# Row gathers over 128 partitions instead of 96 in a two-layer encoder with a product-key expert stage

## What is computed

```python
u = jnp.take(u_tab, idx, axis=0)
act = jax.nn.gelu(jnp.einsum('td,thkd->thk', hb, u))
v = jnp.take(v_tab, idx, axis=0)
return jnp.einsum('thk,thkd->td', gate * act, v)
```

## Time and profile before

| what | value |
|---|---|
| median of 3 runs | 2128.72 us (2105.6, 2128.72, 2135.84) |
| profiled execution, its own time | 2104.95 us |
| its span in the profile | 2103.2 us |
| granted TensorE clock, mean | 0.965 |
| DMA moved | 525.69 MB, mean 250 GB/s |

### The profile page before, as it was taken

How to read it: one execution, slowest core, us unless ns; L and a number is a source line. 1 busy time by engine, 2 the same in 40 slices (tenths; PEclk the granted TensorE clock), 3 DMA queues, 4 the chain that set the end, 5 groups by cost and what they waited for, 6 DMA issues and landing times.

```text
span 2103.2 us, 32369 instructions
## 1 busy us (share of the span) xinstructions
PE 1719.7 (82%) x11548; PEld 1612.4 (77%) x11548; DVE 1224.8 (58%) x2667; ACT 526.5 (25%) x1404; POOL 776.2 (37%) x704
## 2 busy tenths in 40 slices
PE   8999998889966666658999999978799766666667
PEld 6889997779865655657988899978788766666567
DVE  5857986757755444443037668958667644444442
ACT  6854123434400000000047652134444100000000
POOL 6446243334443333331045453333344433333330
PEclk9999999999987988788999999999999999999999
DMA  7250899999999999999831325999999999999996
GB/s 278 81 201 2 269 306 291 292 289 312 309 277 271 281 272 268 274 275 292 279 137 70 132 81 190 287 296 289 289 311 309 294 286 288 289 289 286 279 281 198
DMA packets 143986, 525.69 MB, mean 250 GB/s; under 512 B 18208, under 2 KB 21792, under 8 KB 141472
## 3 DMA queue, kind: packets, MB, share of 16 engines
q1 hardware_dynamic: 86336, 322.57, 50.3%
q0 software_dynamic: 57568, 202.15, 34.9%
HBM read 523.60 MB, written 1.05 MB: 249 GB/s over the span
## 4 chain that ended last, share of the span: by engine, by line
DMA 57%; PE 28%; DVE 10%; ACT 2%; issue 2%; POOL 1%; SPq 0%; DVEq 0%; ACTq 0%; POOLq 0%
PE ps L590 27%; DMA ring<-in_peer_v 25%; DMA nat<-in_peer_v 11%; DMA nat<-in_peer_u 9%; DMA ring<-in_peer_u 8%; DMA grid<-in_u_rows,lists 4%; PE ps L587 1%; DVE grid L1556 1%; DMA grid<-in_w_in 1%; POOL gath_a L574 1%; DVE ab L1528 0%; DVE grid L1516 0%; DVE lists L1525 0%; DVE lists L1520 0%; DVE lists L1532 0%
## 5 line engine op out<-in xcount | busy, mean ns | idle before, releaser
L590 PE MATMUL ps<-grid,ring 128*128 128x160 f32 (+1 forms) x4096 | 632.7, 312 | 175.3 <-DMA ring<-in_peer_v 140.4
L590 PE MATMUL ps<-grid,nat 128*128 128x160 f32 (+1 forms) x4096 | 631.1, 312 | 171.7 <-DMA nat<-in_peer_v 141.2
L590 PEld LDWEIGHTS ps<-grid,ring 128*128 128x128 f32 x4096 | 589.9, 197 | 211.0 <-issue 161.3
L590 PEld LDWEIGHTS ps<-grid,nat 128*128 128x128 f32 x4096 | 588.9, 197 | 207.6 <-issue 172.0
L1612 DVE SCALAR_TENSOR_TENSOR grid<-grid,amount 96x1024 f32<-96x1024 f32 x128 | 163.9, 1281 | 188.5 <-DMA grid<-in_peer_v,lists 188.5
L1612 DVE SCALAR_TENSOR_TENSOR grid<-gath_a,amount,grid 96x1024 f32<-96x1024 f32 x126 | 161.4, 1281 | 188.1 <-DMA gath_a<-in_peer_v,lists 188.1
L574 POOL DMA_INDIRECT gath_a<-in_u_rows,lists x128 | 146.9, 1148 | 280.6 <-DVE dots L1600 207.6
L553 POOL TENSOR_TENSOR wl<-grid,wh 128x512 fp32r<-128x512 f32 (+2 forms) x128 | 142.6, 1140 | 210.4 <-PE ps L590 112.7
L574 POOL DMA_INDIRECT grid<-in_u_rows,lists x128 | 144.7, 1130 | 200.9 <-DVE dots L1600 186.3
L574 POOL DMA_INDIRECT gath_a<-in_peer_v,lists x128 | 119.7, 935 | 232.8 <-DVE grid L1612 209.3
L574 POOL DMA_INDIRECT grid<-in_peer_v,lists x128 | 115.7, 904 | 235.0 <-DVE grid L1612 221.9
(11 more groups left out here) (190 smaller groups left out, 1778.3 us busy)
## 6 DMA issues: line engine op xcount, KB each, us to landing
nat<-in_peer_u SPq DMA_DIRECT2D x128, 512.0 KB, 20.6
ring<-in_peer_u SPq DMA_DIRECT2D x128, 512.0 KB, 20.2
nat<-in_peer_v SPq DMA_DIRECT2D x128, 512.0 KB, 26.4
ring<-in_peer_v SPq DMA_DIRECT2D x128, 512.0 KB, 26.3
grid<-in_peer_wq SPq DMA_DIRECT2D x8, 2048.0 KB, 10.7
grid<-in_w_out SPq DMA_DIRECT2D x2, 4096.0 KB, 13.1
grid<-in_w_in SPq DMA_DIRECT2D x3, 2048.0 KB, 16.5
grid<-in_w_in SPq DMA_DIRECT2D x24, 256.0 KB, 14.4
```

The source lines that it names most:

```text
L590: return nc.tensor.matmul(dst, a, b, start=first, stop=last)
```

## The change

Each gather now fills all 128 partitions. Of the 128 picks of each of the 96 tokens, the first `NR` = 96 are gathered on the token's own partition as before. The last 32 are handed to partitions 96 to 127 (`helpers`): helper partition 96 + i takes the 32 last picks of token i in gathers 0 to 31, of token 32 + i in gathers 32 to 63, of token 64 + i in gathers 64 to 95. So there are 96 gathers of 128 rows for u and 96 for v in a layer, in place of 128 and 128 of 96 rows.

For this the row numbers of the last 32 picks are copied to the helpers (three copies at the end of the picks), the tokens' `xs` rows are copied to the helpers before dots 0, 32 and 64, the gate values likewise in `weigh`, and after additions 31, 63 and 95 the helpers' sums are copied back and added to `x` (`give_back`), the helpers' `acc` being cleared in between. `EARLY_DOTS` stays 24; two dots a round follow in the first 36 rounds of the gate loop and none in the last four.

```diff
+NR = NPK * NS // P
+NH = P - NS
 # gathers (POOL)
-  nc.gpsimd.indirect_dma_start(gath[m % OCT][own, :], None, u_rows if m < NPK else v_rows, bass.IndirectOffsetOnAxis(
-      ap=lists[own, 3, m % NPK:m % NPK + 1].bitcast(U32), axis=0)).then_inc(gath_in[m % OCT], 16)
+  nc.gpsimd.indirect_dma_start(gath[m % OCT], None, u_rows if m < NR else v_rows, bass.IndirectOffsetOnAxis(
+      ap=lists[:, 3, m % NR:m % NR + 1].bitcast(U32), axis=0)).then_inc(gath_in[m % OCT], 16)
-for m in range(2 * NPK):
+for m in range(2 * NR):
 # routing(64) (DVE)
-  v.tensor_copy(lists[own, 3, mine].bitcast(U32), lists[own, 3, mine]).then_inc(picked, 1)
+  ch.step(v.tensor_copy(lists[own, 3, mine].bitcast(U32), lists[own, 3, mine]))
+  for j in range(NS // NH):
+      ins = v.tensor_copy(lists[helpers, 3, j * NH:j * NH + NH].bitcast(U32), lists[j * NH:j * NH + NH, 3, NR:NPK].bitcast(U32))
+  ins.then_inc(picked, 1)
 # dots and additions (DVE)
+def helped(j):
+    if j:
+        dve.wait_ge(gath_used, past[gath_used] + j * NH)
+    ch.step(v.tensor_copy(xs[helpers, :], xs[j * NH:j * NH + NH, :]))
 def dot(n):
+    if n % NH == 0:
+        helped(n // NH)
+def weigh():
+    ch.before()
+    for j in range(NS // NH):
+        ch.did(v.tensor_copy(amount[helpers, j * NH:j * NH + NH], lists[j * NH:j * NH + NH, 0, NR:NPK]))
+    ch.did(v.tensor_copy(amount[own, :], lists[own, 0, 0:NR]))
+    dve.wait_ge(acts_ready, past[acts_ready] + 1)
+    ch.before()
+    ch.step(v.tensor_tensor(amount[:, :], amount[:, :], acts[:, :], ALU.mult))
+def give_back(j):
+    of = slice(j * NH, j * NH + NH)
+    dve.wait_ge(gath_used, past[gath_used] + NR + (j + 1) * NH)
+    ch.step(v.tensor_copy(xs[of, :], acc[helpers, :]))
+    if j < NS // NH - 1:
+        ch.did(v.memset(acc[helpers, :], 0.0))
+    ch.step(v.tensor_tensor(x[of, 0, :], x[of, 0, :], xs[of, :], ALU.add))
 def add_row(n):
+    if n % NH == NH - 1:
+        give_back(n // NH)
 # the gate loop and after it
   for i in range(2):
-      dot(EARLY_DOTS + 2 * m + i)
+      if EARLY_DOTS + 2 * m < NR:
+          dot(EARLY_DOTS + 2 * m + i)
       times_gelu(NA + 2 * m + i, m + 1)
-for n in range(EARLY_DOTS + 2 * NG4, NPK):
-    dot(n)
-dve.wait_ge(acts_ready, past[acts_ready] + 1)
-ch.step(v.tensor_tensor(amount[own, :], acts[own, :], lists[own, 0, 0:NPK], ALU.mult))
-for n in range(NPK):
+weigh()
+for n in range(NR):
     add_row(n)
```

More of the change, by code:

```diff
@@ L204, in build @@
         ikt, jkt, nwkt = (sb(name, [P, SEQ]) for name in ("ikt", "jkt", "nwkt"))
-        dots, acts, amount = (sb(name, [P, NPK]) for name in ("dots", "acts", "amount"))
+        dots, acts, amount = (sb(name, [P, NR]) for name in ("dots", "acts", "amount"))
         ps = ctx.enter_context(nc.psum_tensor("ps", [P, 8, 512], F32))
@@ L256, in build @@
         stat = [ps[:, 3, 384 + 32 * i:416 + 32 * i].rearrange("p (t n) -> p t n", t=NT) for i in range(3)]
-        own = slice(0, NS)
+        own, helpers = slice(0, NS), slice(NS, P)
         xf = part(NK * DT, KD * DT).rearrange("p (k t) -> p k t", k=KD)
@@ L343, in build @@
                 (NK, "prod_done act_stored y_done"),
-                (2 * NPK, "gath_used"),
-                (32 * NPK // OCT, " ".join(f"gath_in{b}" for b in range(OCT))),
+                (2 * NR, "gath_used"),
+                (32 * NR // OCT, " ".join(f"gath_in{b}" for b in range(OCT))),
                 (32 * NO, " ".join(f"nat_in{s}" for s in range(OCT)))):
@@ L1163, in _ @@
                     late_oct(NO - 1)
-                    act.wait_ge(gath_used, past[gath_used] + NPK)
-                    A(acts[own, :], dots[own, :], ACT.Gelu_apprx_tanh).then_inc(acts_ready, 1)
+                    act.wait_ge(gath_used, past[gath_used] + NR)
+                    A(acts[:, :], dots[:, :], ACT.Gelu_apprx_tanh).then_inc(acts_ready, 1)
                     if l == DEPTH - 1:
@@ L1594, in hots @@
                         v.tensor_scalar(hota[:, b, 0, :], iota_ps, of_token(ikt, g, s, 0), of_token(wkt, g, s, 0), ALU.is_equal, ALU.mult).then_inc(hots_ready, 1)
+                    def helped(j):
+                        if j:
+                            dve.wait_ge(gath_used, past[gath_used] + j * NH)
+                        ch.step(v.tensor_copy(xs[helpers, :], xs[j * NH:j * NH + NH, :]))
                     def dot(n):
+                        if n % NH == 0:
+                            helped(n // NH)
                         b = n % OCT
                         dve.wait_ge(gath_in[b], past[gath_in[b]] + 16 * (n // OCT + 1))
-                        v.tensor_tensor_reduce(out=gath[b][own, :], in0=gath[b][own, :], in1=xs[own, :], scale=1.0, scalar=0.0,
-                                               op0=ALU.mult, op1=ALU.add, accum_out=dots[own, n:n + 1]).then_inc(gath_used, 1)
+                        v.tensor_tensor_reduce(out=gath[b], in0=gath[b], in1=xs, scale=1.0, scalar=0.0,
+                                               op0=ALU.mult, op1=ALU.add, accum_out=dots[:, n:n + 1]).then_inc(gath_used, 1)
+                    def weigh():
[13 more added lines that the diff above has]
+                        ch.step(v.tensor_tensor(x[of, 0, :], x[of, 0, :], xs[of, :], ALU.add))
                     def add_row(n):
-                        m = NPK + n
+                        m = NR + n
                         b = m % OCT
@@ L1608, in add_row @@
                         if n == 0:
-                            v.tensor_scalar(acc[own, :], gath[b][own, :], amount[own, 0:1], None, ALU.mult).then_inc(gath_used, 1)
+                            v.tensor_scalar(acc, gath[b], amount[:, 0:1], None, ALU.mult).then_inc(gath_used, 1)
                         else:
                             dve.wait_ge(gath_used, past[gath_used] + m)
-                            v.scalar_tensor_tensor(out=acc[own, :], in0=gath[b][own, :], scalar=amount[own, n:n + 1], in1=acc[own, :],
+                            v.scalar_tensor_tensor(out=acc, in0=gath[b], scalar=amount[:, n:n + 1], in1=acc,
                                                    op0=ALU.mult, op1=ALU.add).then_inc(gath_used, 1)
+                        if n % NH == NH - 1:
+                            give_back(n // NH)
                     def times_gelu(n, groups_done):
@@ L1652, in _ @@
                         for i in range(2):
-                            dot(EARLY_DOTS + 2 * m + i)
+                            if EARLY_DOTS + 2 * m < NR:
+                                dot(EARLY_DOTS + 2 * m + i)
                             times_gelu(NA + 2 * m + i, m + 1)
-                    for n in range(EARLY_DOTS + 2 * NG4, NPK):
-                        dot(n)
-                    dve.wait_ge(acts_ready, past[acts_ready] + 1)
-                    ch.step(v.tensor_tensor(amount[own, :], acts[own, :], lists[own, 0, 0:NPK], ALU.mult))
-                    for n in range(NPK):
+                    weigh()
+                    for n in range(NR):
                         add_row(n)
-                    dve.wait_ge(gath_used, past[gath_used] + 2 * NPK)
                     ch.step(v.tensor_tensor(x[own, 0, :], x[own, 0, :], acc[own, :], ALU.add))
```

## The result

| | before | after |
|---|---|---|
| median of 4 runs | 2125.62 us (2105.60 to 2135.84) | 1731.91 us (1729.95 to 1737.32) |
| ratio, 95% interval | | 0.8161 [0.8098, 0.8225] |
| profiled execution, its own time | 2104.95 us | 1729.95 us |
| span; granted clock, mean | 2103.2 us; 0.965 | 1728.2 us; 0.987 |

The forecast was 2137 us and no change. The kernel became 18% faster, outside the range. From here the page of the changed kernel: busy times, GB/s over the span in 40 slices, and the DMA packets.

The account below looks back on a forecast made before the run. It took two stages per layer as DMA-bound, their ends as PE-bound. Layer 2 +6 us, layer 1 +1 and the picks +1 made +8, added to the median 2128.72: 2137 us, no change, range 2088 to 2185.

Parts of the forecast that it names:

- A gather's pace: Both expert stages: a gather of 144 packets passes with one block, in 3.57 or 3.63 us, taken as 3.6.
- the sign itself: With both queues at work, a rate above 300 GB/s would show the forecast wrong.
- the cost looks like that of the turn: Mixed traffic: blocks' and gathers' rows cost alike, 0.233 and 0.235 us, so turns set the cost; argued against Rival A.
- Rival A: Both queues: gathers over all partitions make alternation cheaper; 2033 us, half of the way to 1930; chance 0.16 with Rival B.
- a sum over the port map: SBUF ports: by the two queues' rates, the fullest port sees about 21 GB/s now and 18 afterwards.
- The law of turns: Block and gather queues: while both wait, they alternate one packet each, at 24.8 ns a turn.
- tails: Layer ends, after the last gathers: blocks left over run alone, about 58 and 34 at 2.2 us each.
- The stretch at 310 GB/s is gone: Gate loop: each round waits for two gathers, 7.2 us for 36 rounds, where one now takes 6.1.
- So no DMA time is lost there: Last four gate-loop rounds: PE takes 21 us while the first 8 v gathers, 29 us of traffic, keep the queue full.
- Rival C: Gate loop: PE's clock falls below 0.75 and PE bounds the rounds; at 0.64, 86 us more, 2223 us; chance 0.07.
- Rival B: Gathers: if each held its queue a fixed time, 128 fewer would pay; inside 12 us; chance 0.16 with Rival A.
- Hidden edits: DVE and POOL: fewer operations gain nothing; added copies, clears and additions cost 15 us a layer if exposed, taken as zero.

Follow-up runs that it names:

- ports: DMA traffic alone, nothing computed: blocks of 128 rows beside gathers or plain loads of various widths; 410 GB/s beside gathers of 128 rows, 287 beside gathers of 96.
- ports2: DMA traffic alone, nothing computed: narrow loads and gathers alone, in turn, or beside blocks; loads on two halves in turn 212 GB/s, one gather in eight narrow 392.
- ports3: DMA traffic alone, nothing computed: plain loads on two queues at once, mostly narrow; 282 GB/s on the two halves, 205 both on the same half.
- pad128: The kernel before, its gathers widened from 96 to 128 partitions with 32 rows that nobody uses; 1834.2 us, ratio 0.8636.
- split96: The changed kernel with each gather made as two DMAs, of 96 and 32 rows; 2185.65 us, ratio 1.0279 to the kernel before.

## Why the prediction was wrong, step by step

**The step that failed** is "A gather's pace", with the sentence "If a turn keeps its cost, it takes 144 x 24.8 = 3.57 us; if the rate of 289 GB/s holds, two times 524288 bytes take 3.63 us. I take 3.6". Neither kept. A turn costs 150/8435 = 17.8 ns, and a pair of gather and block 2 x 524288 / 410 GB/s = 2.56 us. Both ends of that range came from the same row of the same mix, so they bounded nothing: the rate was taken as a property of the engines, where it is one of the shape of what is in flight. With 2.56 in the sums and the rest left alone, the gathers' times of 374 + 310 and 374 + 321 us become 384 x 2.56 = 983, 396 less, and the forecast would have been 1741, 9 us above what was measured. That it comes so close is in part luck: the profiled execution would have been forecast at 2113 - 396 = 1717 and took 1730, 13 more, while the 24 us by which the median of before lay above its profiled execution have only 2 beside them now. The prediction had named the sign itself: a rate above 300 GB/s with both queues at work.

**The inference behind it**: "in the mix the blocks' own rows, which reach every partition, cost as much as the gathers' ... so the cost looks like that of the turn". The row was read rightly (0.233 and 0.235 us), the conclusion wasn't. In `ports` the blocks beside gathers of 96 drop with them although they never changed, and beside gathers of 128 both are fast, with one turn each in both cases. Narrow and wide rows share queues in the engines, and an equal cost of both is just what one slow kind does to the other. The price of blocks alone, 0.197 us a row, was read at a share of 0.85, in a stretch in which they waited for PE.

**Rival A** had the cause and not the size. Its price was 2033, half of the way to its bound of 1930; 1732 came. The bound took 343 GB/s from the stretch at a share of 0.85, scaled up. A better row stood in the trace of before and was overlooked: from 150 to 154 us, ahead of the first gather, blocks alone fill the share (436 of 440 packets are under 8 KB, and queue 0 has none).

```profile
150.00:154.00 4.00, 4.00 (x31) 3.63 (x31) 3.40 (x9) 2.26 (x6) 3.42 (x2) 1.00 1.00 406
```

It is short, but at 406 GB/s a pair takes 2.58 us, and the rival's bound would have been 2137 - 384 x (3.6 - 2.58) = 1745.

Beside its price the rival had a sum over the port map, each queue's bytes divided over the ports that it reaches: the fullest port from 21 to 18, an estimate, a gain of a seventh, where the rate rose from 289 to 410. `ports2` shows why dividing over time falls short: loads on two halves in turn load all ports evenly and still get 212. The Trainium skill says so in "SBUF — State Buffer", "Can I just issue two DMAs to hit both halves?": only one transfer over all 128 partitions reaches all 16 ports. The runs agree as to the full rate (410 against 276 and 286 when split); short of it, two loads at once on the two halves gave 282 in `ports3`, above the 205 of one half. That sentence speaks against the static sum that I made from the map. The likeliest reading is that each engine writes to one port in a transfer of 128 partitions, as the Trainium skill has it in "DMA: Bandwidth & Descriptors", "The descriptor swizzle", and that in a narrower one several engines meet at a port. No trace here says which engine writes where, and it stays a reading.

**The law of turns** held in the v stages, where both queues wait, in the new kernel (8435 and 8433 packets) and in pad128 (8429 and 8430). In the gate loop PE holds the blocks back, and the gathers got 7180 turns to 6870 from 375 to 500 us. What was derived from the law came out too: tails of 56 and 33 blocks at 2.2 us, where 58.5 and 34 were forecast. They depend mainly on the count of turns and little on their price.

**"The stretch at 310 GB/s is gone ... That is what this version pays"** didn't come about. With two gathers in 5.1 us the gate loop isn't bound by DMA any more. DVE in order of time, first and last round of layer 1:

```profile
341.22 0.68 DVE L1662 TENSOR_TENSOR grid<-grid,ps 128x512 f32<-128x512 f32 x1
...
540.10 0.69 DVE L1662 TENSOR_TENSOR grid<-grid,ps 128x512 f32<-128x512 f32 x1 [2.40 <-PE ps L592]
```

That is (540.1 - 341.2)/39 = 5.1 us a round, 204 for 40, with PE busy all the time from 350 us on, where I expected 280. Last additions ended at 760 and 1652 us and not at 948 and 2028. In layer 1, 264 + 192 x 2.56 = 756 comes near, but two deviations cancel in it: in the v stage w_in's short packets take turns as well, so that a gather takes only 150/(9001/144) = 2.40 us, and around the end of the loop DMA time is lost. In layer 2 only the loss is there, and the same sum gives 1137 + 492 = 1629, 23 us too early. After the eighth gather of v all buffers are full until DVE's first addition, behind the loop; POOL's next issue waits 20 us (in layer 1 too), and the DMA share is 0.81 from 1400 to 1425 us:

```profile
1418.88 1.94 POOL L576 DMA_INDIRECT gath_a<-in_peer_v,lists  x1 [19.90 <-DVE grid L1641]
```

So the sentence "So no DMA time is lost there" failed too: it counted on 29 us of traffic from the first 8 gathers, and at 2.56 us each they are 20.

**Rival C** (PE's clock) wasn't put to the test by the changed kernel, since its rounds of 7.2 us never came: the granted clock was 1.00 from 375 to 500 us, and 0.95 in layer 1's v stage with PE busy 83% of the time (123.92 of 150 us), where the earlier trace rows had 0.64 to 0.87 at 62 to 63%. What the forecast had in mind, all partitions filled at the old rate, is nearly `split96`. There the clock did fall, in layer 1 from 340 to 620 us to 0.87, though not below the 0.75 at which the rival's price begins:

```profile
340.00:620.00 280.00, 230.29 (x1497) 218.38 (x1497) 157.44 (x315) 101.11 (x297) 160.97 (x153) 0.87 1.00 273
```

Its profiled execution took 2182 us where the forecast's sum had 2113, with last additions at 993 and 2125 us, and tails of 54 and 23 blocks. So at the old rate too the forecast would have been low, by some 3%. How much of that is the clock, how much the 276 GB/s in place of 289 and how much the second DMA of each gather, no run separates. **Rival B** is not borne out: pad128 keeps all 256 gathers a layer and has most of the gain, and in `ports` a load of 128 rows on 32 partitions has the bytes and the count of DMAs of one on 128, and gives 252 beside blocks where that gives 410.

**Hidden edits** were taken as zero, and no link of the chains above is one of them. DVE in order of time around the first handing back in layer 1's v stage:

```profile
606.56 0.69 DVE L1630 COPY grid<-grid 32x1024 f32<-32x1024 f32 x1
607.51 0.91 DVE L1632 MEMSET grid<- 32x1024 f32 x1 [0.27 <-DVE grid L1630]
608.46 1.21 DVE L1633 TENSOR_TENSOR x<-x,grid 32x1024 f32<-32x1024 f32 x1
```

Copy, clear and addition take 2.8 us (bounds: 1.7 to 3.7), two additions follow from 609.71 on without a wait, and after them DVE waits for the next gather again. The copies at the end of the picks weren't measured by themselves.

## What to carry to other kernels

Where DMA is the bound, and its rows are long as here (4096 bytes), make every DMA into SBUF 128 partitions wide, all of them, since one narrow stream slows its neighbour as much as itself (0.233 against 0.164 us a row): even 32 unused rows in each gather paid, by 286 us. Don't read a full DMA share as a full rate: hold the GB/s of a full stretch against one where only wide DMAs are in flight, be it one of a few microseconds as at 150 us here; if none exists in the trace, measure it before calling a rate fixed. Once the DMAs are fast, look who gets the turns: holding back the queue that is ahead gave another 45 to 60 us (by the ratios, and by the times of two sets of runs).

## What the runs showed of the hardware that was not expected

- 112 partitions are as slow as 96 beside blocks (288 and 287 GB/s). There is no slope from 96 to 112; what lies between 112 and 128 wasn't run.
- Gathers of 96 rows are slower alone (246) than beside blocks of 128 (287). The blocks raise the mean; they are slowed themselves.
- Two loads that share no partition collide when they lie 32 apart (210), as much as two on the same partitions (205).
- Loads on half of the partitions fill the DMA share (1.03) at half the rate: the loss shows as slow packets and not as idle engines. Sixteen partitions gave 109 GB/s at a share of 0.40, which tells nothing of ports: five loads of 64 KB in flight that take 3.0 us each from issue to landing give 109 GB/s by themselves.
- A DMA of 96 rows alone gets 246 to 264 GB/s. If its 64 rows on partitions 0 to 63 went at the 205 of that half and the other 32 beside them, it would get 205 x 96/64 = 307. What takes the rest is open; no run here tells it.
